# Moving the inversion of 16x16 blocks to the sync queue and GpSimd, and storing token rows through four buffers

## What is computed

```python
def step(state, inp):
    r_t, w_t, k_t, v_t, a_t, b_t = inp
    sa = jnp.einsum('bhvk,bhk->bhv', state, a_t)
    state = (state * w_t[:, :, None, :] + sa[..., None] * b_t[:, :, None, :]
             + v_t[..., None] * k_t[:, :, None, :])
    return state, jnp.einsum('bhvk,bhk->bhv', state, r_t)
```

```python
t_mat = lax.linalg.triangular_solve(eye + a_mat, jnp.broadcast_to(eye, a_mat.shape),
                                    left_side=True, lower=True, unit_diagonal=True)
```

## Time and profile before

| what | us |
|---|---|
| median of 3 runs | 2999.83 (2999.08 to 3003.89) |
| the profiled execution, its own time | 2996.28 |
| its span in the trace | 2994.4 |
| PE busy | 2822.2 (94% of the span) |
| DVE busy | 1697.9 (57%) |
| ACT busy | 1219.2 (41%) |
| POOL busy | 14.8 (0%) |

### The profile page before, as it was taken

How to read it: one execution, slowest core, us unless ns; L and a number is a source line. 1 busy time by engine, 2 the same in 40 slices (tenths; PEclk the granted TensorE clock), 3 DMA queues, 4 the chain that set the end, 5 groups by cost and what they waited for, 6 DMA issues and landing times.

```text
span 2994.4 us, 35192 instructions
## 1 busy us (share of the span) xinstructions
PE 2822.2 (94%) x13898; PEld 2242.3 (75%) x13898; DVE 1697.9 (57%) x2465; ACT 1219.2 (41%) x1900; POOL 14.8 (0%) x22
## 2 busy tenths in 40 slices
PE   8989899999999998999999999999878899969997
PEld 6667778888886666788888887776666788858885
DVE  4475455555335565455554335457864545469995
ACT  3333334332222342333322225455536243348873
POOL 0000000000000000000000000000000000000000
PEclk9999999999999999999999999999989999979999
DMA  4112123223332122132233331111110112459981
GB/s 169 57 46 67 43 65 105 92 98 97 97 118 71 46 64 57 36 102 92 99 99 113 99 99 64 57 64 57 50 48 30 50 43 98 154 211 386 390 318 54
DMA packets 96179, 307.22 MB, mean 103 GB/s; under 512 B 25744, under 2 KB 31760, under 8 KB 84240
## 3 DMA queue, kind: packets, MB, share of 16 engines
q1 hardware_dynamic: 69056, 284.88, 27.6%
q10 hardware_dynamic: 24368, 10.66, 1.3%
q0 software_dynamic: 2592, 9.44, 0.9%
HBM read 296.03 MB, written 8.91 MB: 102 GB/s over the span
## 4 chain that ended last, share of the span: by engine, by line
PE 82%; DVE 8%; ACT 4%; issue 3%; DMA 2%; ACTq 1%; POOL 0%; SPq 0%; POOLq 0%; DVEq 0%
PE bank L368 20%; PE bank L370 20%; PE bank L369 20%; PE bank L363 2%; PE bank L365 2%; PE bank L364 2%; PE bank L1935 1%; DVE dn L1818 1%; DVE flow_rest L398 1%; ACT flow_head L387 1%; PE bank L1235 1%; PE bank L2600 1%; PE bank L1069 1%; ACTq L1148 0%; ACT L418 0%
## 5 line engine op out<-in xcount | busy, mean ns | idle before, releaser
L368 PE MATMUL bank<-h_head,flow_head 128*128 128x512 f32 x2144 | 888.7, 415 | 34.8 <-DVE flow_rest L398 27.1
L370 PE MATMUL bank<-h_head,flow_rest 128*128 128x512 f32 x2144 | 843.0, 393 | 0.0
L369 PE MATMUL bank<-h_rest,flow_head 128*128 128x512 f32 x2144 | 842.9, 393 | 0.0
L387 ACT ACTIVATE flow_head<-flow_raw 128x1024 fp32r<-128x1024 f32 (+2 forms) x372 | 379.6, 1021 | 920.9 <-PE bank L370 877.4
L398 DVE TENSOR_TENSOR flow_rest<-flow_raw,flow_head 128x1024 fp32r<-128x1024 f32 (+2 forms) x372 | 437.9, 1177 | 308.2 <-ACT flow_head L387 307.1
L368 PEld LDWEIGHTS bank<-h_head,flow_head 128*128 128x128 f32 x2144 | 407.5, 190 | 151.9 <-issue 60.5
L369 PEld LDWEIGHTS bank<-h_rest,flow_head 128*128 128x128 f32 x2144 | 408.0, 190 | 88.4 <-issue 13.3
L370 PEld LDWEIGHTS bank<-h_head,flow_rest 128*128 128x128 f32 x2144 | 406.7, 190 | 88.0
L368 PE MATMUL bank<-ff_head,flow_head 128*128 128x512 f32 x352 | 136.9, 389 | 0.0
L369 PE MATMUL bank<-ff_rest,flow_head 128*128 128x512 f32 x352 | 136.9, 389 | 0.0
L370 PE MATMUL bank<-ff_head,flow_rest 128*128 128x512 f32 x352 | 136.9, 389 | 0.0
(11 more groups left out here) (605 smaller groups left out, 4074.1 us busy)
## 6 DMA issues: line engine op xcount, KB each, us to landing
flow_raw<-in_w_in SPq DMA_DIRECT2D x176, 512.0 KB, 3.3
ring<-in_experts SPq DMA_DIRECT2D x84, 1024.0 KB, 7.4
flow_raw<-in_w_gate_up SPq DMA_DIRECT2D x88, 512.0 KB, 3.3
flow_raw<-in_w_down SPq DMA_DIRECT2D x32, 512.0 KB, 3.5
flow_raw<-in_w_out SPq DMA_DIRECT2D x24, 512.0 KB, 3.3
flow_raw<-in_paths SPq DMA_DIRECT2D x24, 256.0 KB, 2.6
flow_raw<-in_w_down SPq DMA_DIRECT2D x16, 384.0 KB, 3.1
flow_raw<-in_path_b SPq DMA_DIRECT2D x8, 512.0 KB, 3.3
```

The costliest lines, as they stand in the source:

```text
L368: nc.tensor.matmul(ps[u.bank][:, :], wh[:, c:c + P], head, start=start, stop=False)
L369: nc.tensor.matmul(ps[u.bank][:, :], wh[:, c:c + P], rest, start=False, stop=False)
L370: last = nc.tensor.matmul(ps[u.bank][:, :], wr[:, c:c + P], head, start=False, stop=stop)
L387: nc.scalar.activation(self.parts_of[p.slot][0][:, 0:p.words], p.raw, ACT.Copy).then_inc(self.heads, 1)
```

## The change

`base_inverse` no longer puts anything into the queues of ACT and DVE. Its transfers go into the sync queue, in two groups (`to_lanes` and `from_lanes`) that `loads` writes ahead of two chosen pieces of the stream: the first group ahead of the first piece whose first column has the tick `at(0) + 8` or a later one, the second group two pieces further on. The memsets and the 30 steps go to GpSimd, which had no work until the gathers. All calls of `flow.act` and `flow.dve` inside `base_inverse` go away with the parts that they stood in; `rwkv_inverse` and `delta_inverse`, with their wait on `blocks_landed`, stay as they are. The token rows get four buffers and four semaphores, so ACT waits from c = 4 on, for the store of chunk c - 4.

```diff
@@ -237,7 +237,7 @@
     def __init__(self, nc, sems, ps, raw, w_head, w_rest):
         self.nc, self.ps, self.raw = nc, ps, raw
         self.parts_of = [(w_head[:, n], w_rest[:, n]) for n in range(2)]
-        self.pieces, self.blocks, self.units = [], [], []
+        self.pieces, self.blocks, self.units, self.block_of, self.before_block = [], [], [], [], {}
...
@@ -249,6 +249,7 @@
         mark.up(16)
         words = src.shape[-1]
         raw = self.raw[:, k % RAW_SLOTS, 0:words]
+        self.block_of.append(len(self.blocks))
         self.blocks.append((raw, src, mark.sem, [k - RAW_SLOTS] if k >= RAW_SLOTS else [], None))
         self.pieces.append(Piece(raw, words, (mark.sem, mark.total), k % 2))
         return k
@@ -260,6 +261,7 @@
         self.blocks.append((dst[:, :], src, mark.sem, used, first))
         out = []
         for n, slot in enumerate(slots):
+            self.block_of.append(len(self.blocks) - 1)
             self.pieces.append(Piece(dst[:, n * 1024:(n + 1) * 1024], 1024, (mark.sem, mark.total), slot))
             out.append(len(self.pieces) - 1)
         return out
@@ -325,9 +327,17 @@
     def dve(self, t):
         self.run("dve", t)
 
+    def piece_at(self, t):
+        return next(n for n, p in enumerate(self.pieces) if p.first >= t)
+
+    def ahead_of(self, piece, transfers):
+        self.before_block[self.block_of[piece]] = transfers
+
     def loads(self):
         sp = self.nc.sync
-        for dst, src, landed, used, first in self.blocks:
+        for n, (dst, src, landed, used, first) in enumerate(self.blocks):
+            if n in self.before_block:
+                self.before_block[n](sp)
             if used:
                 sp.wait_ge(self.heads, max(used) + 1)
                 sp.wait_ge(self.rests, max(used) + 1)
@@ -1124,39 +1134,47 @@
 
...
-    nc, flow, v, a = k.nc, k.flow, k.v, k.a
+    nc, flow, g_p = k.nc, k.flow, k.nc.gpsimd
     given, solved, term = (spare[:, m * 256:m * 256 + BASE * BASE] for m in range(3))
     blocks_left, lanes_landed, lanes_left, blocks_landed, cleared, steps, done = k.marks(
         "base_away", "base_in", "base_back", "base_out", "base_cleared", "base_steps", "base_done")
     g, x = (t.rearrange("p (i j) -> p i j", j=BASE) for t in (given, solved))
 
-    def scalar_part():
-        flow.act(at(0))
+    blocks_left.up(16 * P // BASE)
+    lanes_landed.up(16)
+    lanes_left.up(16)
+    blocks_landed.up(16 * P // BASE)
+    all_left, lanes_in, lanes_back, all_landed = (
+        blocks_left.at(16 * P // BASE), lanes_landed.at(16), lanes_left.at(16), blocks_landed.at(16 * P // BASE))
+    all_solved = done.at(1)
+
+    def to_lanes(sp):
         for needs in lows_ready:
-            a.wait_ge(*needs)
+            sp.wait_ge(*needs)
         for b in range(P // BASE):
-            a.dma_start(dram["blocks"][b].rearrange("u i j -> i u j"), base_blocks(low, b)).then_inc(*blocks_left.up(16))
-        flow.act(at(.2))
-        a.wait_ge(*blocks_left.at(16 * P // BASE))
-        a.dma_start(given, dram["blocks"].rearrange("b u i j -> (b u) (i j)")).then_inc(*lanes_landed.up(16))
-        flow.act(at(.6))
-        a.wait_ge(*done.at(1))
-        a.dma_start(dram["blocks_back"].rearrange("b u i j -> (b u) (i j)"), solved).then_inc(*lanes_left.up(16))
-        flow.act(at(.8))
-        a.wait_ge(*lanes_left.at(16))
+            sp.dma_start(dram["blocks"][b].rearrange("u i j -> i u j"), base_blocks(low, b)).then_inc(all_left[0], 16)
+        sp.wait_ge(*all_left)
+        sp.dma_start(given, dram["blocks"].rearrange("b u i j -> (b u) (i j)")).then_inc(lanes_in[0], 16)
+
+    def from_lanes(sp):
+        sp.wait_ge(*all_solved)
+        sp.dma_start(dram["blocks_back"].rearrange("b u i j -> (b u) (i j)"), solved).then_inc(lanes_back[0], 16)
+        sp.wait_ge(*lanes_back)
         for b in range(P // BASE):
-            a.dma_start(base_blocks(low, b), dram["blocks_back"][b].rearrange("u i j -> i u j")).then_inc(*blocks_landed.up(16))
-        flow.act(at(1))
-
-    def vector_part():
-        flow.dve(at(0))
+            sp.dma_start(base_blocks(low, b), dram["blocks_back"][b].rearrange("u i j -> i u j")).then_inc(all_landed[0], 16)
+
+    piece = flow.piece_at(at(0) + 8)
+    flow.ahead_of(piece, to_lanes)
+    flow.ahead_of(piece + 2, from_lanes)
+
+    def gpsimd_part():
         for needs in lows_ready:
-            v.wait_ge(*needs)
-        k.dve_chain(nc.vector.memset(solved, 0.0))
-        nc.vector.memset(solved[:, 0:BASE * BASE:BASE + 1], 1.0).then_inc(*cleared.up())
-        flow.dve(at(.4))
-        v.wait_ge(*cleared.at(1))
-        v.wait_ge(*lanes_landed.at(16))
+            g_p.wait_ge(*needs)
+        nc.gpsimd.memset(solved, 0.0).then_inc(*cleared.up())
+        g_p.wait_ge(*cleared.at(1))
+        nc.gpsimd.memset(solved[:, 0:BASE * BASE:BASE + 1], 1.0).then_inc(*cleared.up())
+        g_p.wait_ge(*cleared.at(2))
+        g_p.wait_ge(*lanes_in)
         for j in range(BASE - 1):
             m, n = BASE - 1 - j, j + 1
             if turned:
@@ -1167,19 +1185,17 @@
                 t = term[:, 0:m * n].rearrange("p (i k) -> p i k", k=n)
                 left, right, to = (g[:, n:BASE, j:j + 1].to_broadcast([P, m, n]), x[:, j:j + 1, 0:n].to_broadcast([P, m, n]),
                                    x[:, n:BASE, 0:n])
-            nc.vector.tensor_tensor(t, left, right, ALU.mult).then_inc(*steps.up())
-            v.wait_ge(*steps.at(2 * j + 1))
-            ins = nc.vector.tensor_tensor(to, to, t, ALU.add)
+            nc.gpsimd.tensor_tensor(t, left, right, ALU.mult).then_inc(*steps.up())
+            g_p.wait_ge(*steps.at(2 * j + 1))
+            ins = nc.gpsimd.tensor_tensor(to, to, t, ALU.add)
             if j < BASE - 2:
                 ins.then_inc(*steps.up())
-                v.wait_ge(*steps.at(2 * j + 2))
+                g_p.wait_ge(*steps.at(2 * j + 2))
             else:
                 ins.then_inc(*done.up())
-        flow.dve(at(1))
-
-    scalar_part()
-    vector_part()
-    return blocks_landed.at(16 * P // BASE)
+
+    gpsimd_part()
+    return all_landed
 
 
...
-    k.tokens = [at(f"tokens_{n}", c, (NT, P)) for n, c in enumerate((46, 47))]
+    k.tokens = [at(f"tokens_{n}", c, (NT, P)) for n, c in enumerate((46, 47, 68, 69))]
...
-    k.router_landed, k.stored = k.loaded.over(48), [k.table_a.over(32), k.table_2.over(64)]
+    k.router_landed, k.stored = k.loaded.over(48), [k.table_a.over(32), k.table_2.over(64), k.first_landed.over(32)]
+    k.signals["dg_split"] = Mark(sems, "dg_split")
+    k.stored += [k.signals["dg_split"].over(2)]
...
     def store(a, m):
         a.wait_ge(flow.products, flow.units[m].done)
-        if c >= 2:
-            a.wait_ge(*k.stored[c % 2].at(16 * (c // 2)))
-        nc.scalar.activation(k.tokens[c % 2][:, :, :], k.ps[b][:, :].rearrange("p (t n) -> p t n", n=P), ACT.Copy).then_inc(
+        if c >= 4:
+            a.wait_ge(*k.stored[c % 4].at(16))
+        nc.scalar.activation(k.tokens[c % 4][:, :, :], k.ps[b][:, :].rearrange("p (t n) -> p t n", n=P), ACT.Copy).then_inc(
             *k.late["tokens_kept"].up())
         a.wait_ge(*k.late["tokens_kept"].at(c + 1))
-        a.dma_start(dram["h_rows"].rearrange("(t p) d -> p t d", p=P)[:, :, c * P:(c + 1) * P], k.tokens[c % 2][:, :, :]).then_inc(
-            *k.stored[c % 2].up(16))
+        a.dma_start(dram["h_rows"].rearrange("(t p) d -> p t d", p=P)[:, :, c * P:(c + 1) * P], k.tokens[c % 4][:, :, :]).then_inc(
+            *k.stored[c % 4].up(16))
...
     for m in k.stored:
-        g.wait_ge(*m.at(64))
+        g.wait_ge(*m.at(32))
```

## The result

| | before | after |
|---|---|---|
| median, us | 3000.48 (2999.08 to 3003.89, 4 runs) | 3031.91 (3026.09 to 3038.62, 4 runs) |
| the profiled execution, its span | 2994.4 | 3028.2 |
| first transfer of the blocks to the inverse, places 1 to 4 | 25.0, 24.5, 23.9, 24.9 | 35.5, 35.5, 35.2, 35.0 |
| first token rows to the first gather | 58.5 | 50.3 |

The change makes the kernel slower: ratio 1.0108, with an interval of 1.0095 to 1.0121, some 31 us. I had predicted 3069 with a range of 3038 to 3120.

What follows compares the result with a forecast made beforehand. The prediction took PE's queue to bound the kernel (82% of the chain that ended last). Later inverses (75.2 us), the clock (+2) and the token rows (-8.2) sum to +69.0 on 2999.8: 3069 us, range 3038 to 3120.

Steps and rivals of the forecast that it cites:

- DVE's wait at the front: At the four inverses, DVE waits directly behind the step ahead; PE stands still for the whole trip, about 30 us each.
- The step of a GpSimd instruction: In the blocks' trip at each inverse, 30 GpSimd steps at 0.55 us each, 16.5 us in all.
- the 75.2 us: Sum by which the four inverses begin later: 20.6, 20.6, 19.3 and 14.7 us, all on the path.
- Rival (a): GpSimd's step costs near DVE's, 0.24 to 0.35 us, giving 3032 to 3045 us; chance 0.13.
- From the blocks' return to the inverse: After the trip DVE makes up postponed work: 14.0 us in places 1 and 2, 12.3 in 3, 8.5 in 4.
- The trip without the steps: The blocks' transfers out to HBM and back at the four inverses: 15.1, 14.6, 14.4 and 14.6 us.
- The clock: Longer PE idling at the inverses moves the slow start to the stream's products: +2 us, between -4 and +8.
- The sync queue at nothing: Stream loads held back behind the blocks' transfers, up to 30 us late, cost nothing because DVE's stop covers them.
- The token rows: Between token rows and first gather, four buffers remove ACT's wait for a store: -8.2 us, at least -5.
- (c): Held-back loads do matter: DVE and ACT stop ahead of place 1, each place loses another 5 us, 3089; chance 0.05.
- (d): DVE's early wait costs nothing: 3029 us (chance 0.03), or 2992 with the step at DVE's price (0.02).

Runs made afterwards that it cites:

- e4: The changed kernel with each of the 15 multiplications of a place done twice on GpSimd; 3054.1 us.
- e1: The changed kernel with one call `flow.dve(at(1))` put back behind the GpSimd steps, so DVE waits late again; 3009.6 us.
- e12: The changed kernel with twelve extra VectorE products of constant tables ahead of DVE's wait, in each place; 3051.4 us.
- e7: e6 with the two groups of transfers moved down among the stream's loads; 2985.8 us.
- e6: e2 with only the 18 transfers moved to the sync queue as the change does it, steps on VectorE, DVE's wait late; 2999.8 us.
- e2: The kernel before with only the four buffers for token rows; 2986.3 us, ratio 0.9953.

## Why the prediction was wrong

**DVE's wait at the front: right.** The order of the queue said where it would stand, and DVE and PE stood for 20.5 to 24.7 us on the rows named. e4 shows that each microsecond of the trip costs about one there, and e1 that the wait's place is the cause.

**The step of a GpSimd instruction: the term that failed.** I took 0.55 us, 16.5 for 30. From the first step's start to the transfer behind the last one it is 10.5 us in each place, 0.35 each, the very edge of what I had called the forecast. That is 24.0 of the 75.2 us. The lower bound, DVE's 0.24, was the row of the same operation; I moved away from it toward the gather's 1.07 us, which is the row of another instruction (DMA_INDIRECT) and told nothing of a product of 60 elements. Rival (a), with 0.13, had the right price at its upper end and gives 3045, still 13 above the result. The sentence of the Trainium skill, page "GPSIMD Engine Reference", section "Engine selection" (about twice as slow) would have given 0.48, an estimate by that page. Measured beside a DVE that stands still it is 1.46 times DVE's step, beside a busy one three times (a step every 0.73 us in e12).

**From the blocks' return to the inverse: mis-sized in places 1 and 2.** I had 14.0 us, and it was 10.8. The row "from PE's start to the eviction, 305.90 to 316.04" was misread: DVE was inside its 30 small steps until then, so the eviction at 316.04 was late by DVE's own occupation and not by PE. After, it is 8.7 from PE's start (324.21 to 332.93), though that holds six products of `yh` that PE had behind it at 305.90 before; from the first product with `h_head`, at 326.94, it is 6.0, where I had 10.1. Further, PE did not need the 2.5 us of eviction, rest and eviction: it had stopped at a bank, went on 0.74 us after the return, and the head of its next piece was already made. Place 3 had 10.3 instead of 12.3, place 4 10.3 instead of 8.5. Together 6.6 us.

**The trip without the steps** was 14.2, 14.2, 14.4 and 14.2 us instead of the 58.7 in sum that I had, 1.7 us less. With 24.0 and 6.6 that is 32.3, and 75.2 less 32.3 is the 42.9 measured.

**The clock** (+2) did not show: the same products took 4.4 us less than before (2817.8 against 2822.2), and the sum without the term is already 0.9 us above the difference of the spans. The slow start moved as foretold (first product 0.80 us after 22.9 idle).

**The sync queue at nothing: right for this kernel, for the reason given.** ACT waited for a held-back load, 6.43 us at place 3 and 7.99 at place 4, and nobody waited for ACT, since DVE stood still. With that cover gone the held-back loads cost 14 us from e7 to e6, 10.0 of them PE's idle time; "a few microseconds in each place" is what I had written for that case.

**The token rows: right.** Predicted 8.2, found 8.2 at the place. The gather did not wait for the last store.

**Rivals.** (c), held-back loads at 0.05, is out for this kernel. In (d) I gave 3029 for the case that DVE does not stop; e1 is that case and took 3009.6: I had counted a trip longer by 9.3 us in each place, and from the first transfer to the inverse it was 1.0, 1.4, 5.7 and 1.6 longer than before.

## What to carry to other kernels

A call that only writes out due work, such as `flow.dve(at(1))`, is also what decides where the next wait stands; take its block away and the wait moves up over work that had covered it. Here one such line is worth 22 of the 31 us lost.

Before work goes to GpSimd, ask what VectorE does at that time, with its operands in SBUF, and whether anybody waits for the chain: here 30 dependent steps cost 10.3 us alone, 15.0 beside a busy VectorE, and 7.0 on VectorE itself (from the first step's start to the last one's). In a distance read from a timeline, look what the engine that ends it was doing, before it is used as the price of another.

## What the runs showed that I had not expected

- A GpSimd step that starts beside a VectorE operation with both inputs in SBUF lasts until just behind that operation's end: 0.65 us beside one of 0.69, 1.15 beside one of 1.29, 0.2 to 0.3 alone. VectorE's own operation is slowed by some 0.1 us at most (1.29 against 1.22; `dn<-sgf,dn` 0.78 against 0.68).
- The same 13898 products took 2812.0 us in one kernel and 2834.6 in another, each read from one profiled run. 9.2 us gained in the four places (e7 against e2) did not show in the time; the stretch between places 3 and 4 alone was 4.7 us longer for the same matmuls, at a mean granted clock of 0.90 instead of 0.95. Before a difference of this size is put down to a wait, PE's idle time and its busy time have to be read separately.
- Two sound halves are better than the change as a whole: the buffers alone give 2986.3, and with the transfers in the sync queue at the right loads, the steps left on VectorE and a wider stretch 2979.7, 0.7% below the kernel before.
